# The first expert pass takes its tokens from SBUF by one-hot products, and constant products fill the routing waits

## The chip, the cores and the metric

One Trainium2 chip, one core. The time is the device time of the kernel in microseconds (us). On the core, TensorE (PE in the profile, its weight loads PEld) multiplies, VectorE (DVE), ScalarE (ACT) and GpSimd (POOL) do the rest, and SyncE (SP) issues most of the DMAs. TensorE's clock is granted at one of two levels, 1.2 or 2.4 GHz; the profile writes them as 0.50 and 1.00.

## What is computed

One layer for 512 tokens of width 1024, all in fp32: three branches (an RWKV-7 recurrence, a spatial gating unit, a convolution) are mixed, added to the input and normalised. Each token then goes to the two best of 32 experts.

```python
x = layer_norm(ALPHA * x + merged @ w_out[l], ln1_g[l], ln1_b[l])   # "x1" in the kernel
scores = sigmoid(x @ router_w)                                      # 512 x 32
# the best of 4 groups of 8 experts, in it the 2 best experts; gate = their scores, normed to 1
h = silu(xblk @ w_gate[e]) * (xblk @ w_up[e])                       # 1024 -> 512, for the tokens of expert e
y[token] += gate * (h @ w_down[e])                                  # 512 -> 1024
x = layer_norm(ALPHA * x + y, ln2_g[l], ln2_b[l])
```

## The kernel before

The program is written engine by engine, with semaphores, and each engine runs its instructions in the order in which they are written. The change touches the stretch between the branches and the experts, some 50 us long.

**Weights.** The experts' weights are 6 MB for each of 32 experts, cut into six chunks of 1 MB (four of gate and up, two of down). There are four sets of six places in SBUF; expert e uses set e mod 4. SP issues the loads in a fixed order. The loads of experts 0 to 3 (`load`, L410) go out as their places come free. The last four of them are chunks 0 and 1 of expert 3 (places in `ring`, where x1 lies too), which wait until x1 has been stored to DRAM (`x1_stored`), and chunks 4 and 5 of expert 2, which wait for the tables (`tables_ready`, s_tab). Behind them stands the loop of the other 28 experts (`reload`, L446): the chunk of expert e + 4 goes out when TensorE has used the same chunk of expert e (`w_used`).

**Residual, norm and router.** For each of four tiles c of 128 tokens TensorE forms the mixed rows (`mix`, L1372: 16 products of 512 columns), VectorE adds, normalises and leaves x1 in `ring` (L959 to L972), TensorE transposes it (`turn_x1`, L1381), ScalarE copies the transpose out of PSUM (L693) and stores x1 to DRAM, and TensorE forms the scores (`router`, L1388: 8 products of 32 columns). In the profile each fp32 product is two records of PE, each transpose one.

**Routing.** VectorE chooses the experts (L984 to L1010). TensorE then counts for each token how many before it chose the same expert (the rank products, L1409 and L1410). VectorE turns the ranks into pass and slot numbers (L1043 to L1064) and builds one-hot tables (L1070 to L1075). TensorE multiplies these (the table products, L1417), and VectorE writes the tables of token rows, result rows and gates (L1080 to L1082), which sets `tables_ready`.

**Passes.** A pass takes up to 64 tokens of one expert; there is one for each expert and one more for each further 64 tokens. GpSimd gathers the tokens of pass p from DRAM into `xe` by an indirect DMA (`gather`, L524 and L527), always one pass ahead. TensorE transposes them (`turn`, L1426), VectorE copies them to `xeT` (`turned`, L1095), TensorE does gate and up (L1437, 32 records), transposes of h (L1446) and down (L1457, 16 records), and GpSimd scatters the result (L541). The transposes of pass p + 1 stand on TensorE behind gate and up of pass p and ahead of the transposes of h. Pass 0 has its own `gather(0)` and `turn(0)`, and behind `turn(0)` TensorE reads the pass numbers of the first expert from SBUF (two register loads) and branches into the loop.

Of the kernel before, what the change touches and what calls it, by code (L numbers as in the profile page):

```python
# [10 lines left out]
ALU = mybir.AluOpType  # L11
ACT = mybir.ActivationFunctionType
AX_X = mybir.AxisListType.X
ADD, SUB, MUL, MAX = ALU.add, ALU.subtract, ALU.mult, ALU.max


P = 128
T, D = 512, 1024
KT = D // P
TT = T // P  # L20
# [135 lines left out]
def program(nc, x_tok, xT, w_in, par, table, lora, rows, sgu_b, sgu_wT, w_o, w_out, router_w, zeros, w_gu, w_down, out):  # L156
    with ExitStack() as ctx:
# [24 lines left out]
        def C(name):  # L182
            at, n = CONSTS[name]
            return const[:, at:at + n]
# [115 lines left out]
        def late(where, flat, n):  # L300
            at = place[where]
            place[where] += n
            return flat[:, at:at + n]
# [8 lines left out]
        slot_hot = late("late", late_sb, 8 * P).rearrange("p (n s) -> p n s", n=8)  # L312
        assert place["late"] <= 2 * RW + 2 * T
        chosen = late("raw", raw_flat, (TT + 1) * N_EXP).rearrange("p (c e) -> p c e", c=TT + 1)
        small = late("raw", raw_flat, 12 * TOPK * TT).rearrange("p (i n) -> p i n", i=12)
# [44 lines left out]
        s_begun, s_more = map(sem, ["gathers_begun", "further_passes_ready"])  # L360
        s_first, s_x1back, s_lnback = map(sem, ["first_passes_ready", "x1_back", "ln2_rows_in"])
        s_x1st, s_rw = sem("x1_stored"), sem("router_par_in")
# [13 lines left out]
        def _(sp):  # L376
# [54 lines left out]
            load(3, 3, 3)  # L431
            sp.wait_ge(s_x1st, 16 * TT)
            for c in (0, 1):
                load(3, c, 3)
# [35 lines left out]
        def _(pool):  # L470
# [51 lines left out]
            def gather(p):  # L522

                pool.tensor_copy(idx_now[:, 0:1], idx_tab[:, bass.ds(p, 1)]).then_inc(s_idx, 1)  # L524
                pool.wait_ge(s_idx, p + 1)
                pool.sem_inc(s_begun, 1)
                pool.indirect_dma_start(xe, None, x1_dram, bass.IndirectOffsetOnAxis(ap=idx_now[:, 0:1], axis=0),  # L527
                                        bounds_check=last_half_row, oob_is_err=False).then_inc(s_xe, 16)

            def next_tokens(p):  # L530
                pool.wait_ge(s_xe, p * 16 + 16)
                pool.wait_ge(s_xeTp, p + 1)
                gather(p + 1)
# [14 lines left out]

            gather(0)
            next_tokens(0)  # L550
            next_tokens(1)
# [9 lines left out]
            scatter(more + (N_EXP - 1))  # L561
            pool.wait_ge(s_xe, more * 16 + 16 * (N_EXP + 1))

# [165 lines left out]
        def _(dve):  # L729
# [280 lines left out]
            dve.tensor_tensor(chosen[:, 1:, :], hot[:, 0, :, :], hot[:, 1, :, :], ADD).then_inc(s_chosen, 1)  # L1010

            KC = TOPK * TT
            row_base = small[:, 0, 4:5]
# [26 lines left out]
            dve.wait_ge(s_rank, 1)  # L1040
            rank_ps = bank[:, 5, 0:TT * N_EXP].rearrange("p (c e) -> p c e", c=TT)
            for k in range(TOPK):
                ins = dve.tensor_tensor(work4[:, k, :, :], hot[:, k, :, :], rank_ps, MUL)  # L1043
# [19 lines left out]
            dve.tensor_copy(extra_i[:, :], count[:, EXTRA, :])  # L1063
            dve.tensor_copy(first_i[:, :], count[:, FIRST, :]).then_inc(s_first, 1)  # L1064


# [25 lines left out]

            def turned(p):
                dve.wait_ge(s_xeTp, p + 1)
                dve.tensor_copy(xeT, bank[:, 2, :].rearrange("p (c s) -> p c s", c=4)).then_inc(s_xeT, 1)  # L1095

            turned(0)
            with dve.Fori(0, N_EXP) as i:
# [36 lines left out]
        def _(pe):  # L1135
# [249 lines left out]
            def router(c):  # L1385
                pe.wait_ge(s_x1T, c + 1)
                for k in range(KT):
                    ins = pe.matmul(bank[:, 4, c * N_EXP:(c + 1) * N_EXP], x1T[:, c % 2, k, :], rw_sb[:, k, :],  # L1388
                                    start=(k == 0), stop=(k == KT - 1))
                if c == TT - 1:  # L1390
                    ins.then_inc(s_scp, 1)
# [4 lines left out]
            pe.wait_ge(s_m3, KT)  # L1396
            pe.wait_ge(s_rw, 32)
            for c in range(TT):
                if c + 1 < TT:
                    mix(c + 1)  # L1400
                if c:
                    router(c - 1)
                turn_x1(c)
            router(TT - 1)

            pe.wait_ge(s_chosen, 1)

            for n in range(TT + 1, 1, -1):
                pe.matmul(bank[:, 5, (TT + 1 - n) * N_EXP:(TT + 1) * N_EXP], C("ones"), chosen[:, 0:n, :], start=(n == TT + 1), stop=False)  # L1409
            pe.matmul(bank[:, 5, 0:TT * N_EXP], C("earlier"), chosen[:, 1:, :], start=False, stop=True).then_inc(s_rank, 1)  # L1410

            for n in range(TOPK * TT):
# [5 lines left out]
            ins.then_inc(s_tabp, 1)  # L1418
            pe.wait_ge(s_tab, 1)

            def turn(p):

                pe.wait_ge(s_xe, p * 16 + 16)
                pe.wait_ge(s_xeT, p)
                for c in range(4):
                    ins = pe.transpose(bank[:, 2, c * P:(c + 1) * P], xe[:, c * P:(c + 1) * P], C("ident"))  # L1426
                ins.then_inc(s_xeTp, 1)
# [34 lines left out]

            turn(0)
            pe.wait_ge(s_first, 1)
# [69 lines left out]
```

## Time and profile before

| | us |
|---|---|
| median of 3 runs | 1132.33 (1131.18 to 1133.24) |
| profiled execution | 1133.84 |
| its span, first to last instruction | 1132.1 |
| PE busy in the span | 990.2 (87%) |
| DVE busy | 359.3 (32%) |
| DMA: moved in the span | 261.35 MB, mean 231 GB/s |

What lies around the span is 1133.84 - 1132.1 = 1.74 us. Three things are to be read in the profile. The view by windows gives for a stretch how busy each engine was, the granted clock and what the DMA engines moved; where they move about 420 GB/s they are never idle. The chain of waits gives, back from the last instruction, what each piece waited for. The timeline gives each engine's instructions in order. An idle engine costs nothing unless the chain runs over it.

### The profile page before, as it was taken

How to read it: one execution, taken by the hardware profiler on the slowest of the kernel's cores; microseconds unless marked ns; L12 is line 12 of the kernel's file. 1: busy time of each engine (PE TensorE's matmuls, PEld its weight loads, DVE VectorE, ACT ScalarE, POOL GpSimd, SP SyncE). 2: the span in 40 equal slices, each digit the busy share in tenths (PEclk: the TensorE clock that was granted, in tenths of full speed). 3: DMA queues.
4: the chain of work that ended last, by engine and by line, in shares of the span. 5: the costliest groups of instructions: out<-in, count | busy, mean ns of one | idle time of the engine just before them, and what ended most of it. 6: DMA issues, size and time to landing. Idle time of an engine off the chain costs nothing.

```text
span 1132.1 us, 15272 instructions
## 1 busy us (share of the span) xinstructions
PE 990.2 (87%) x5900; PEld 458.8 (41%) x5901; DVE 359.3 (32%) x672; ACT 166.6 (15%) x302; POOL 123.9 (11%) x192
## 2 busy tenths in 40 slices
PE   7999999999999999999994588988888888887740
PEld 3634466466457447444454133333333333322210
DVE  0694452463363363322445000001100000000018
ACT  1113312321322132200000000000000100000010
POOL 1000010010010010033000112111211121111100
PEclk9999999999999999999995799999999999999985
DMA  8222211220220220573628699999999999999982
GB/s 252 61 74 56 75 39 39 58 55 20 75 57 21 56 56 2 171 297 153 258 83 344 219 416 419 403 419 420 419 419 420 419 419 419 419 420 420 421 322 117
DMA packets 90190, 261.35 MB, mean 231 GB/s; under 512 B 11080, under 2 KB 56136, under 8 KB 65312
## 3 DMA queue, kind: packets, MB, share of 16 engines
q1 hardware_dynamic: 83776, 249.46, 57.0%
q0 software_dynamic: 5648, 9.07, 2.2%
q10 hardware_dynamic: 720, 2.15, 0.5%
q8 instruction: 36, 0.59, 0.2%
q14 instruction: 10, 0.08, 0.0%
HBM read 256.97 MB, written 12.85 MB: 238 GB/s over the span
## 4 chain that ended last, share of the span: by engine, by line
PE 65%; DVE 15%; SPq 9%; DMA 5%; issue 4%; ACT 2%; DVEq 0%; ACTq 0%; POOLq 0%; PEldq 0%
PE bank L1437 14%; PE proj L1192 11%; SPq L446 9%; PE proj L1156 9%; PE bank L1457 7%; PE proj L1372 5%; PE bank L1282 5%; PE bank L1360 5%; DVE arena L760 4%; DMA arena<-w_gu 3%; DMA gates<-y_rows 2%; PE proj L1164 2%; DVE arena L1095 1%; DVE arena L845 1%; PE bank L1321 1%
## 5 line engine op out<-in xcount | busy, mean ns | idle before, releaser
L1192 PE MATMUL proj<-xT_sb,ring 128*128 128x512 f32 x384 | 182.1, 607 | 0.0
L1088 DVE TENSOR_TENSOR const<-pass_sb,bank 128x256 f32<-128x256 f32 x33 | 13.9, 422 | 408.3 <-ACT pass_sb L704 408.3
L1437 PE MATMUL bank<-arena 128*64 128x512 f32 x544 | 122.2, 596 | 15.7 <-PE bank L1457 11.1
L1156 PE MATMUL proj<-xT_sb,ring 128*128 128x512 f32 (+2 forms) x288 | 126.0, 594 | 0.0
L1192 PEld LDWEIGHTS proj<-xT_sb,ring 128*128 128x128 f32 x384 | 68.3, 189 | 68.3 <-issue 64.8
L1156 PEld LDWEIGHTS proj<-xT_sb,ring 128*128 128x128 f32 (+2 forms) x288 | 52.9, 185 | 71.6 <-issue 71.5
L1437 PEld LDWEIGHTS bank<-arena 128*64 128x64 f32 x544 | 43.0, 137 | 94.7 <-issue 82.8
L1437 PE MATMUL bank<-gates,arena 128*64 128x512 f32 x256 | 59.8, 617 | 8.6 <-PE bank L1457 4.7
L1282 PEld LDWEIGHTS bank<-arena 64*64 64x64 f32 x1536 | 52.8, 134 | 18.2 <-ACT arena L662 9.1
L1282 PE MATMUL bank<-arena 64*64 64x64 f32 (+1 forms) x1536 | 56.5, 228 | 0.0
L1360 PE MATMUL bank<-branches,arena 128*128 128x512 f32 x128 | 55.4, 593 | 0.9 <-DVE branches L939 0.9
L1457 PE MATMUL bank<-arena,const 128*64 128x512 f32 x208 | 48.4, 600 | 8.8 <-DVE const L1091 8.8
L1372 PE MATMUL proj<-arena 128*128 128x512 f32 x128 | 55.4, 592 | 0.0
L541 POOL DMA_INDIRECT y_rows<-const,raw x33 | 33.7, 1020 | 147.8 <-ACT const L708 147.8
L704 ACT ACTIVATE pass_sb<-bank 128x256 f32<-128x256 f32 x33 | 12.7, 384 | 249.5 <-PE bank L1437 249.5
L708 ACT ACTIVATE const<-bank,raw 128x512 f32<-128x512 f32 x33 | 22.7, 687 | 178.7 <-PE bank L1457 178.7
L760 DVE SCALAR_TENSOR_TENSOR arena<-arena,par_sb 128x512 f32<-128x512 f32 x60 | 39.8, 749 | 0.0
L527 POOL DMA_INDIRECT pass_sb<-x_rows,raw x34 | 35.8, 1052 | 26.9 <-POOL raw L524 24.6
L524 POOL COPY raw<-raw 128x1 int32 (+1 forms) x34 | 6.2, 183 | 296.4 <-PE bank L1426 207.2
L1437 PEld LDWEIGHTS bank<-gates,arena 128*64 128x64 f32 x256 | 18.5, 141 | 49.4 <-issue 43.2
L1360 PEld LDWEIGHTS bank<-branches,arena 128*128 128x128 f32 x128 | 24.2, 190 | 31.9 <-issue 30.1
L662 ACT ACTIVATE arena<-bank 128x256 f32<-128x256 f32 (+1 forms) x64 | 27.5, 437 | 64.6 <-PE bank L1282 59.6
(255 smaller groups left out, 1016.5 us busy)
## 6 DMA issues: line engine op xcount, KB each, us to landing
arena<-w_gu SPq DMA_DIRECT2D x64, 1024.0 KB, 24.6
gates<-w_gu SPq DMA_DIRECT2D x32, 1024.0 KB, 21.7
arena<-w_down SPq DMA_DIRECT2D x24, 1024.0 KB, 24.6
ring<-w_in SPq DMA_DIRECT2D x42, 512.0 KB, 3.9
gates<-w_down SPq DMA_DIRECT2D x16, 1024.0 KB, 23.6
branches<-w_down SPq DMA_DIRECT2D x16, 1024.0 KB, 26.7
xT_sb<-w_gu SPq DMA_DIRECT2D x16, 1024.0 KB, 26.0
ring<-w_gu SPq DMA_DIRECT2D x16, 1024.0 KB, 25.1
```

The costliest lines, as they stand in the source:

```text
L446: sp.dma_start(w_chunk[b][c], src.rearrange("a p n -> (a p) n")).then_inc(s_w[b][c], 16)
L527: pool.indirect_dma_start(xe, None, x1_dram, bass.IndirectOffsetOnAxis(ap=idx_now[:, 0:1], axis=0), bounds_check=last_half_row, oob_is_err ...
L541: pool.indirect_dma_start(y_dram, bass.IndirectOffsetOnAxis(ap=row_now[:, 0:1], axis=0), y_e, None, bounds_check=last_row, oob_is_err=Fals ...
L662: ins = act.activation(d, bank[:, 3 * g + b, 0:TT * n].rearrange("p (j n) -> p j n", j=TT), ACT.Copy)
L760: ins = dve.scalar_tensor_tensor(conv_acc[:, i, :], src, w, conv_acc[:, i, :], MUL, ADD)
L1156: ins = pe.matmul(proj[0:w, b, :], ring[:, slot, k, 0:w], xT_sb[:, k, :], start=(k == 0), stop=(k == KT - 1))
L1192: ins = pe.matmul(proj[:, gate_at["bank"], :], ring[:, gate_at["slot"], k, :], xT_sb[:, k, :], start=(k == 0), stop=(k == KT - 1))
L1282: ins = pe.matmul(bank[t, 3 * g + b, j * n:j * n + n], lhsT[t, j, :], rhs[t, j, :], start=True, stop=True)
L1360: ins = pe.matmul(bank[:, 3 * (m % 2) + n, :], wo_sb[:, k0 + k, m * P:(m + 1) * P], src[:, k, :], start=(k == 0), stop=(k == nk - 1))
L1372: ins = pe.matmul(proj[:, n % 2, :], merged[:, k, c * P:(c + 1) * P], wout_sb[:, k, T * i:T * i + T], start=(k == 0), stop=(k == KT - 1))
L1437: ins = pe.matmul(bank[SLOTS * h:SLOTS * h + SLOTS, 0, :], xeT[:, k % 4, SLOTS * (k // 4):SLOTS * (k // 4) + SLOTS], gu[k // 2][:, k % 2, ...
L1457: ins = pe.matmul(bank[SLOTS * h:SLOTS * h + SLOTS, 1, :], hT[:, f % 2, SLOTS * (f // 2):SLOTS * (f // 2) + SLOTS], wd[f // 2][:, f % 2, h ...
```

## The change

VectorE builds for each tile of 128 tokens a one-hot matrix `first_hot` (128 tokens by 64 slots) as soon as the rank products are there: a token has its one where its rank equals the slot, if it chose expert 0. TensorE multiplies x1, still in `ring`, by it: 8 blocks of 128 channels by 4 tiles, 32 products of 64 columns, which add up in the PSUM bank from which `turned(0)` copies. So `gather(0)`, `turn(0)` and TensorE's wait for the tables ahead of it are gone; `gather(1)` is the first. `turned(0)` moves on VectorE from behind the tables to a place ahead of the pass and slot one-hots, whose space `first_hot` shares. SP's loads of chunks 0 and 1 of expert 3, which overwrite x1, now also wait for the end of the new products (s_xeTp).

`keep_clock(n)` is n products of the identity by 512 constant columns into a free PSUM bank. There are 2 ahead of the last `turn_x1` (behind a wait for `residual_added`, since the bank holds mixed rows), 8 behind the last `router`, and 4 behind the new products.

```diff
+        first_hot = slot_hot[:, 6:8, :].rearrange("p n s -> p (n s)").rearrange("p (c s) -> p c s", c=TT)
...
             sp.wait_ge(s_x1st, 16 * TT)
+            sp.wait_ge(s_xeTp, 1)
             for c in (0, 1):
                 load(3, c, 3)
...
-                pool.wait_ge(s_idx, p + 1)
+                pool.wait_ge(s_idx, p)
...
-            gather(0)
-            next_tokens(0)
+            gather(1)
             next_tokens(1)
             scatter(0)
...
             rank_ps = bank[:, 5, 0:TT * N_EXP].rearrange("p (c e) -> p c e", c=TT)
+            for c in range(TT):
+                dve.tensor_scalar(first_hot[:, c, :], C("slot_iota")[:, 0:SLOTS], rank_ps[:, c, 0:1], chosen[:, 1 + c, 0:1],
+                                  ALU.is_equal, MUL).then_inc(s_firsthot, 1)
...
             dve.tensor_copy(first_i[:, :], count[:, FIRST, :]).then_inc(s_first, 1)
+            turned(0)
...
-            turned(0)
             with dve.Fori(0, N_EXP) as i:
...
+            def keep_clock(n):
+
+                for _ in range(n):
+                    pe.matmul(proj[:, 0, :], C("ident"), const[:, 0:T], start=True, stop=True)
+
             for c in range(TT):
                 if c + 1 < TT:
                     mix(c + 1)
                 if c:
                     router(c - 1)
+                if c == TT - 1:
+                    pe.wait_ge(s_pre, 2 * TT)
+                    keep_clock(2)
                 turn_x1(c)
             router(TT - 1)
+            keep_clock(8)
...
             pe.matmul(bank[:, 5, 0:TT * N_EXP], C("earlier"), chosen[:, 1:, :], start=False, stop=True).then_inc(s_rank, 1)
+
+            for c in range(TT):
+                pe.wait_ge(s_firsthot, c + 1)
+                for k in range(KT):
+                    at = (k % 4) * P + SLOTS * (k // 4)
+                    ins = pe.matmul(bank[:, 2, at:at + SLOTS], x1[:, c, k * P:(k + 1) * P], first_hot[:, c, :],
+                                    start=(c == 0 and k == 0), stop=(c == TT - 1 and k == KT - 1))
+            ins.then_inc(s_xeTp, 1)
+            keep_clock(4)
...
             ins.then_inc(s_tabp, 1)
-            pe.wait_ge(s_tab, 1)
...
-                pe.wait_ge(s_xe, p * 16 + 16)
+                pe.wait_ge(s_xe, p * 16)
...
-            turn(0)
             pe.wait_ge(s_first, 1)
```

TensorE from the last transposes of x1 to the passes, before (the number behind L is the line, `bank` and `proj` are PSUM, x counts instructions that read alike, and the brackets name the semaphores waited for):

```order
L1381 MATMUL bank<-const,ring 128x128 [waits x1T_out,x1_ready]
L1381 MATMUL bank<-const,ring 128x128 x7
L1388 MATMUL bank<-late_sb,xT_sb 128x32 [waits x1T_out]
L1388 MATMUL bank<-late_sb,xT_sb 128x32 x7
L1409 MATMUL bank<-raw,const 128x160 [waits chosen_ready]
...
L1410 MATMUL bank<-raw,const 128x128
L1417 MATMUL bank<-arena,late_sb 128x144 [waits scores_ready,one_hots_ready]
...
L1426 MATMUL bank<-const,pass_sb 128x128 [waits xeT_out,tokens_in,tables_ready]
L1426 MATMUL bank<-const,pass_sb 128x128 x3
L1477 UNCONDITIONAL_BRANCH [waits first_passes_ready]
```

The same place now (L1385, L1392, L1422, L1423 and L1439 are the old L1381, L1388, L1409, L1410 and L1417):

```order
L1405 MATMUL proj<-const 128x512 [waits residual_added]
L1405 MATMUL proj<-const 128x512
L1385 MATMUL bank<-const,ring 128x128 [waits x1T_out,x1_ready]
...
L1392 MATMUL bank<-late_sb,xT_sb 128x32 x7
L1405 MATMUL proj<-const 128x512 x8
L1422 MATMUL bank<-raw,const 128x160 [waits chosen_ready]
...
L1423 MATMUL bank<-raw,const 128x128
L1429 MATMUL bank<-late_sb,ring 128x64 [waits first_slots_ready]
...
L1405 MATMUL proj<-const 128x512 x4
L1439 MATMUL bank<-arena,late_sb 128x144 [waits scores_ready,one_hots_ready]
```

The new products (L1429) and the 4 fill products stand between the rank products and the table products, and no transposes of gathered tokens stand ahead of the branch any more.

SP's loads between the last router and the loop, before:

```order
L410 DMA xT_sb<-w_gu 128x2048 [waits scores_in_psum]
L410 DMA ring<-w_gu 128x2048 [waits x1_stored]
L410 DMA ring<-w_gu 128x2048
L410 DMA arena<-w_down 128x2048 [waits tables_ready]
L410 DMA late_sb<-w_down 128x2048
```

and now:

```order
L411 DMA xT_sb<-w_gu 128x2048 [waits scores_in_psum]
L411 DMA ring<-w_gu 128x2048 [waits xeT_psum,x1_stored]
L411 DMA ring<-w_gu 128x2048
L411 DMA arena<-w_down 128x2048 [waits tables_ready]
L411 DMA late_sb<-w_down 128x2048
```

The order of the loads is the same; the two of `ring` have one more wait.

## Rows read from the trace of the kernel before

**Rows 1.** Windows: start:end, length, busy us (x records), clock, DMA share, GB/s.

```profile
617.00:624.00 7.00, 4.19 (x16) 3.86 (x16) 3.56 (x12) 0.04 (x1) 0.00 (x0) 0.56 0.06 26
624.00:631.00 7.00, 0.00 (x0) 0.00 (x0) 0.00 (x0) 1.45 (x2) 1.32 (x2) 0.68 0.84 311
631.00:640.00 9.00, 5.81 (x16) 2.23 (x18) 0.69 (x1) 0.00 (x0) 1.24 (x2) 0.50 0.06 19
640.00:652.00 12.00, 10.26 (x48) 3.36 (x46) 1.38 (x3) 1.16 (x3) 1.44 (x4) 0.99 0.98 353
652.00:718.00 66.00, 58.45 (x272) 21.30 (x270) 6.88 (x15) 5.23 (x14) 12.25 (x20) 1.00 1.01 419
718.00:724.00 6.00, 6.00 (x31) 1.87 (x26) 0.00 (x0) 0.59 (x2) 1.01 (x1) 1.00 0.92 324
```

**Rows 2.** Timeline of TensorE: start, length, what, idle before it; first wait for weights.

```profile
1002.40 1.94 PE L1437 MATMUL bank<-arena 128*64 128x512 f32 x8 [0.34 <-DMA arena<-w_gu]
```

**Rows 3.** Timeline of SP's queue around routing and at expert 9's loads.

```profile
604.99 0.81 SPq L410 DMA_DIRECT2D ring<-w_gu  x2
623.88 0.33 SPq L410 DMA_DIRECT2D arena<-w_down  x1
...
639.15 7.19 SPq L446 DMA_DIRECT2D gates<-w_gu  x4
...
719.48 3.75 SPq L446 DMA_DIRECT2D arena<-w_gu  x3
```

**Rows 4.** Chain of waits, mixing to the third pass: start, us, what.

```profile
571.94 1.70 PE bank L1388 x16
...
574.55 13.75 PE proj L1372 x32
...
592.01 3.31 PE bank L1388 x16
595.33 1.77 PE bank L1381 x8
...
598.20 3.63 PE bank L1388 x16
...
609.74 2.08 PE bank L1409 x8
611.81 0.55 PE bank L1410 x2
...
616.56 0.47 DVE arena L1070
...
619.07 4.21 PE bank L1417 x16
...
623.87 8.46 issue
632.33 1.10 PE bank L1426 x4
...
633.45 0.70 DVE arena L1095
...
635.27 9.53 PE bank L1437 x32
...
651.20 7.10 PE bank L1437 x32
...
664.68 7.10 PE bank L1437 x32
```

**Rows 5.** Windows again, cut where the granted clock changes (columns as Rows 1).

```profile
588.00:592.40 4.40, 3.29 (x29) 2.92 (x27) 3.63 (x8) 1.16 (x2) 0.00 (x0) 1.00 0.71 249
592.40:616.00 23.60, 10.91 (x49) 10.08 (x48) 14.04 (x66) 2.58 (x3) 0.00 (x0) 0.50 1.01 417
...
623.10:626.50 3.40, 0.16 (x1) 0.00 (x0) 0.62 (x4) 1.49 (x2) 1.32 (x2) 1.00 0.45 101
```

**Rows 6.** Line 527, the 34 gathers of tokens, issue to landing.

```profile
DMA to landing us min/median/max: 3.4/6.7/7.6
```

More of the change, by code:

```diff
@@ L360, in program @@
         s_begun, s_more = map(sem, ["gathers_begun", "further_passes_ready"])
-        s_first, s_x1back, s_lnback = map(sem, ["first_passes_ready", "x1_back", "ln2_rows_in"])
+        s_firsthot, s_first, s_x1back, s_lnback = map(sem, ["first_slots_ready", "first_passes_ready", "x1_back", "ln2_rows_in"])
         s_x1st, s_rw = sem("x1_stored"), sem("router_par_in")
@@ L530, in next_tokens @@
             def next_tokens(p):
-                pool.wait_ge(s_xe, p * 16 + 16)
+                pool.wait_ge(s_xe, p * 16)
                 pool.wait_ge(s_xeTp, p + 1)
@@ L561, in _ @@
             scatter(more + (N_EXP - 1))
-            pool.wait_ge(s_xe, more * 16 + 16 * (N_EXP + 1))
+            pool.wait_ge(s_xe, more * 16 + 16 * N_EXP)
         @block.scalar
@@ L1010, in _, with turned @@
             dve.tensor_tensor(chosen[:, 1:, :], hot[:, 0, :, :], hot[:, 1, :, :], ADD).then_inc(s_chosen, 1)
+            def turned(p):
+                dve.wait_ge(s_xeTp, p + 1)
+                dve.tensor_copy(xeT, bank[:, 2, :].rearrange("p (c s) -> p c s", c=4)).then_inc(s_xeT, 1)
             KC = TOPK * TT
@@ L1091, in one_pass @@
                 dve.tensor_copy(hT, bank[:, 3, 0:FE // 2].rearrange("p (c s) -> p c s", c=2)).then_inc(s_hT, 1)
-            def turned(p):
-                dve.wait_ge(s_xeTp, p + 1)
-                dve.tensor_copy(xeT, bank[:, 2, :].rearrange("p (c s) -> p c s", c=4)).then_inc(s_xeT, 1)
-            turned(0)
             with dve.Fori(0, N_EXP) as i:
```

## The prediction

> **What bounds the kernel now.** I read three views in this order: the windows, to find where the DMA engines rest; the timelines of TensorE and of SP, to find who waits for whom in the passes; and the chain of waits, for the length of each step of the routing.
>
> From 652 us on the windows show 419 GB/s, which is as fast as this kernel's loads ever go; I call 420 full rate [rows 1]. TensorE waits for weights for the first time at 1002.40 us, and then in nearly every pass [rows 2]. Until then it is ahead, but its lead is only used up by a stream that never rests. So the end is set by the weights: bytes left, divided by 420 GB/s, plus every microsecond in which the DMA engines rest before the stream closes up. That is the quantity to sum. A TensorE that starts its passes earlier gains nothing by that itself; it gains by letting SP issue the reloads earlier.
>
> Rest before, as the missing part of each window: 617 to 624, 7 x (1 - 26/420) = 6.6; 624 to 631, 7 x (1 - 311/420) = 1.8; 631 to 640, 9 x (1 - 19/420) = 8.6; 640 to 652, 12 x (1 - 353/420) = 1.9. Together 18.9 us. Later there is one dip, 718 to 724: 6 x (1 - 324/420) = 1.4, where SP gets leave for expert 9's first chunk only at 719.48 [rows 1, 3]. All are TensorE's doing: the loads of `ring` go out at 604.99 and are through at about 617.4, the next two wait for the tables (623.88), and the first reload waits until the first pass has used its first chunk, at 639.15, 3.9 us after that pass began [rows 3, 4].
>
> **The change, step by step (times of the profiled execution).**
>
> 1. Two fill products ahead of the last transposes. A product of 512 columns is 13.75/16 = 0.86 us at 2.4 GHz (32 records are 16 products) and twice that, 1.72, at 1.2; the router shows the factor, 1.70 us for 16 records before the fall and 3.63 after it [rows 4]. The clock fell at 592.4 [rows 5], behind 4.1 us (the mixing ends at 574.55 + 13.75 = 588.3) in which TensorE did router products, transposes and a wait, and nothing of the change lies ahead of that. So the two products come cold, at 595.33, when the transposes could have gone: they cost 3.4 us on the chain. If they bring the clock back, the transposes (1.77) and the last router (3.63) halve, and 3.4 - 0.9 - 1.9 = +0.6 is left. Between +0.6 and +3.4 there is no row that decides: the one rise in this stretch came at 623.1, behind 4.0 us of table products, and these are 3.4 us. I take the middle, +2.0.
>
> 2. Eight fill products. The wait that hides them is 609.74 - 601.83 = 7.9 us (the last router ends at 598.20 + 3.63) [rows 4]. At 2.4 GHz they take 6.9 and are covered. If they start cold and the clock comes after about 4.4 us (4.0 us at the table products; in the first pass it came by about 640, some 4.8 us in), they take 4.4 + 4.7 = 9.1, so 1.2 are not covered. All cold: 13.7, which is rival B. The rank products then run at 2.4 GHz, 2.08 + 0.55 halved, -1.3. Ends for the rank products' end, 612.36 before: warm 0.6 - 1.3 = -0.7; cold 3.4 + 1.2 - 1.3 = +3.3. Middle +1.3: 613.7.
>
> 3. The new products. VectorE needs about 0.3 us for the first one-hot of 128 x 64 (an estimate, under the 0.47 of L1070's 128 x 384). 32 products are 64 records with a weight load of 128 x 128 each, as in the router; by its rows 64 x 1.70/16 = 6.8 us at 2.4 GHz and 64 x 3.63/16 = 14.5 at 1.2 [rows 4]. I take 6.8, as the eight fill products have just run: done at 613.7 + 0.3 + 6.8 = 620.8. VectorE's own chain to L1064 (612.36 to 616.56, plus under 1 us for the one-hots) lies beside it. The Trainium skill, TensorE: Matmul & The Clock Gate, section Back-to-back issue gap, gives about 81 ns for each matmul in a stream of weight loads and matmuls at 128 columns; no row here is that short (106 ns for 32 columns). By it the products would take 5.2 us and the forecast below would be 1.6 us lower.
>
> 4. VectorE now waits for them at `turned(0)`, and its pass and slot one-hots queue behind. From the end of the products: copy 0.7, then from L1070 to the table products, 619.07 - 616.56 = 2.5, so 3.2 us [rows 4]. The four fill products (3.4 us) lie beside this and end 0.2 later, at 624.2. The table products, 16 records in 4.21 at 1.2 GHz, take 2.1 at 2.4: end 626.3, tables ready 0.6 later at 626.9 (before 623.88, so 3.0 later).
>
> 5. The first pass. `gather(0)`, 8.46 us from tables to tokens, and `turn(0)`, 1.10, are gone [rows 4]. What stays is reading the pass numbers and branching: 635.27 - 633.43 = 1.8 us before, some of it perhaps beside the table products now; between 0 and 1.8 I take 0.9. Start 627.2 instead of 635.27: 8.1 us earlier. And warm: before, the first pass took 651.20 - 635.27 = 15.9 and the second 664.68 - 651.20 = 13.5, so 2.4 less [rows 4]. But its last part waits for `gather(1)`, which only starts at the tables: 626.9 + 8.5 = 635.4, against 627.2 + 7.1 = 634.3, some 1.0 us late. TensorE is then 8.1 + 2.4 - 1.0 = 9.5 us ahead of the old trace in all later passes. The landing times (3.4 to 7.6, median 6.7) [rows 6] leave up to 0.9 more wait.
>    The Trainium skill, DMA: Bandwidth & Descriptors, section Anatomy of one DMA, gives about 2.0 us plus bytes/436 GB/s for a DMA of GpSimd; 0.26 MB would be 2.6 us, and `gather(1)` would land before it is wanted. The trace says 6.7 [rows 6]; by the page the forecast would be about 0.5 lower.
>
> 6. The DMA engines. The two `ring` loads (2.1 MB, 5.0 us) leave their old place, so the queue is dry at 617.4 - 5.0 = 612.4. They now go out at 620.8, and bytes flow some 1.6 us behind an issue (1.8 us of rest in 624 to 631, the window that begins at the issue of 623.88 [rows 1, 3]): rest 622.4 - 612.4 = 10.0. They are through at 627.4; the next two, issued at 626.9, flow at 628.5: 1.1 more. They last till 633.5, and the first reload is issued 653.31 - 651.20 = 2.1 us into a warm pass, at 629.3: no more rest. Total 11.1 instead of 18.9, and 0.6 us of work less (one gather of 0.26 MB): the stream is 8.4 us ahead. At expert 9 SP gets leave at 719.48 - 9.5 = 710.0, and the queue runs dry at about 719.4 - 8.4 = 711.0; before, the two coincided. With the 1.6 us of flow some 0.6 of the dip is left: 0.8 more. Sum 9.2 us.
>
> Own time of the profiled execution 1133.84 - 9.2 = 1124.6 (span 1122.9); it stood 1.5 above the median 1132.33, so the median is **1123.1**. With the warm end of steps 1 and 2 everything after is 2.0 earlier, 1121.1; with the cold end 1125.1.
>
> **The rivals.**
>
> A. The clock falls again within the new products: half the time of each of their records is weight load, and the fall at 592.4 came behind 4.1 us of like work [rows 5]. Against it: those 4.1 us held waits and transposes, and the new products follow eight dense ones without a gap. If it falls 4 us in, the other 2.8 double (+2.8) and the four fill products start cold (+2.2). Products end 623.6, tables 631.9; rest 12.8 + 3.3 = 16.1; stream ahead 18.9 - 16.1 + 0.6 = 3.4, dip 0.7: **1128.2**.
>
> B. The other side: the fill fails to raise the clock, or not before the new products. The place is the eight fill products: at 1.2 GHz they take 13.7 against a cover of 7.9, and nothing behind them on TensorE can pass. With all cold: rank products end 612.36 + 3.4 + 5.8 = 621.6, the new ones 636.4, then 6.9 and 4.2: tables 648.1, rest 25.6 + 6.7 = 32.3: **1145**. If only the new products are cold (+7.7, fill +2.5): rest 17.7 + 3.6, **1133** to 1135. It decides where the new products end later than about 630 (620.8 + 9.2). For it: the clock stood at 1.2 from 592.4 to 623.1 with 11 of 23.6 us busy [rows 5]. Against it: table products and gate/up products did raise it.
>
> C. It does not do what it says, as the DMA engines are not earlier: the loads of `ring`, held until x1 is used, rest as long as the gather did. This is the sum of step 6 with another end, and it needs the products to end after 629: TensorE would be ahead and the stream would not. **1131** to 1132.
>
> **How the numbers follow.** Main case 0.70: 1123.1, its own range 1121 to 1125 widened by 0.5 for the dip, the branch and the gather. A 0.14, 1128. C, with the cold-products half of B, 0.07, 1131 to 1134. B, slower, 0.09, 1135 to 1145. The range 1120.5 to 1129.5 takes in the main case and A. A measurement of this kernel can tell 0.2% (2.3 us) from no change: faster (under 1130.1) 0.84, same 0.07, slower 0.09.
>
> **What would show it.** In the new profile: two L1405 products between 595 and 599 that delay the transposes; the clock back at 2.4 before the rank products; L1429, 64 records in about 7 us, ending at 619 to 623; the first pass at about 627, 7.1 us long in gate and up; a short wait ahead of the transposes of pass 1; DMA rest between 612 and 622 and none between 631 and 640; the dip at 720 nearly gone; first wait for weights still near 1000. It would be wrong if L1429 takes over 10 us, if the first pass starts after 632, or if the DMA engines rest a second time behind 630.

## The result, and the profile after

The change makes the kernel 0.5% faster: 1127.67 us, the median of 7 times from 1122.5 to 1131.47, against 1132.09, the median of 7 from 1130.62 to 1133.24; the ratio is 0.995 with a 95% interval of 0.993 to 0.9971. That is 4.4 us, half of the 9.2 forecast. It is inside the stated range, but outside the main case's own range of 1121 to 1125: the median falls in a group that the range takes in only because it was drawn wide enough for rival A. That it hit the range is luck. The times of the changed kernel are not spread evenly. They lie in three groups, and the mean granted clock of each execution goes with them: three at 1122.5 to 1123.8 (clock 0.981), three at 1127.7 to 1127.9 (0.976 to 0.977), one at 1131.5 (0.973). The profiled execution took 1123.78 us with a span of 1122.0, so it belongs to the first group: it shows the change at its best, 10.1 us under the span before.

TensorE's timeline in it (start, length, what, idle before it):

```profile
591.71 1.97 PE L1392 MATMUL bank<-late_sb,xT_sb 128*128 128x32 f32 x16 [1.11 <-ACT xT_sb L694]
593.51 3.30 PE L1405 MATMUL proj<-const 128*128 128x512 f32 x4
596.61 1.43 PE L1385 MATMUL bank<-const,ring 128*128 128x128 f32 x8
599.15 2.13 PE L1392 MATMUL bank<-late_sb,xT_sb 128*128 128x32 f32 x16 [1.11 <-ACT xT_sb L694]
601.09 8.67 PE L1405 MATMUL proj<-const 128*128 128x512 f32 x16
609.60 1.05 PE L1422 MATMUL bank<-raw,const 128*128 128x160 f32 x8
...
611.50 7.36 PE L1429 MATMUL bank<-late_sb,ring 128*128 128x64 f32 x64 [0.58 <-DVE late_sb L1048]
618.70 3.65 PE L1405 MATMUL proj<-const 128*128 128x512 f32 x8
622.19 2.14 PE L1439 MATMUL bank<-arena,late_sb 128*128 128x144 f32 x16
626.02 7.09 PE L1458 MATMUL bank<-gates,arena 128*64 128x512 f32 x32 [1.69 <-issue]
633.88 0.66 PE L1447 MATMUL bank<-const,pass_sb 128*128 128x128 f32 x4 [0.78 <-DMA pass_sb<-x_rows,raw]
```

Against [rows 4]: the first pass starts at 626.02 instead of 635.27 and its gate and up take 7.1 us instead of 9.5; its transposes wait 0.78 us for the gather. The new products (L1429) take 7.4 us. SP's queue in the same execution:

```profile
618.96 0.80 SPq L411 DMA_DIRECT2D ring<-w_gu  x2
624.95 0.33 SPq L411 DMA_DIRECT2D arena<-w_down  x1
...
628.15 6.50 SPq L448 DMA_DIRECT2D gates<-w_gu  x4
...
708.37 6.51 SPq L448 DMA_DIRECT2D arena<-w_gu  x4
```

And its windows (columns as in [rows 1]):

```profile
612.00:620.00 8.00, 8.00 (x65) 7.33 (x65) 4.97 (x20) 0.00 (x0) 0.00 (x0) 1.00 0.07 19
620.00:624.00 4.00, 4.00 (x21) 2.66 (x20) 2.98 (x8) 0.00 (x0) 0.00 (x0) 1.00 0.94 354
624.00:628.00 4.00, 2.31 (x13) 0.91 (x13) 0.62 (x4) 1.49 (x2) 1.32 (x2) 1.00 0.88 295
628.00:640.00 12.00, 9.63 (x46) 3.19 (x43) 1.44 (x3) 1.03 (x3) 1.43 (x3) 1.00 1.01 421
640.00:708.00 68.00, 60.57 (x278) 23.48 (x280) 6.89 (x15) 5.94 (x17) 12.28 (x20) 1.00 1.02 418
```

There is one hole left in the DMA stream, 612 to 620, where [rows 1] had two, 617 to 624 and 631 to 640. From 628 on it is closed. The first reload is issued at 628.15, 11.0 us earlier than in [rows 3], and expert 9's at 708.37 instead of 719.48.

### The profile page after: what moved, and what is told of

Read it like the earlier page. It is cut to its first block, busy times and chain, and to the rows that moved or that the text cites. A ratio compares the mean times of both kernels' runs of the same rounds, so it can differ in the third digit from the quotient of the medians.

```text
span 1122.0 us, 15417 instructions
## 1 busy us (share of the span) xinstructions
PE 1001.1 (89%) x5988; PEld 469.4 (42%) x5989; DVE 360.3 (32%) x676; ACT 166.4 (15%) x302; POOL 122.6 (11%) x190
## 4 chain that ended last, share of the span: by engine, by line
PE 68%; DVE 15%; DMA 6%; SPq 6%; issue 3%; ACT 2%; DVEq 0%; POOLq 0%; POOL 0%; ACTq 0%
PE bank L1458 16%; PE proj L1196 11%; PE proj L1160 9%; PE bank L1478 9%; SPq L448 5%; PE proj L1376 5%; PE bank L1286 5%; PE bank L1364 5%; DVE arena L761 4%; DMA arena<-w_gu 3%; DVE arena L1015 2%; DMA gates<-y_rows 2%; PE proj L1168 1%; DVE arena L846 1%; ACT pass_sb L705 1%
## 5 line engine op out<-in xcount | busy, mean ns | idle before, releaser
L1097 DVE TENSOR_TENSOR const<-pass_sb,bank 128x256 f32<-128x256 f32 x33 | 13.9, 421 | 406.8 <-ACT pass_sb L705 406.8
L1458 PE MATMUL bank<-arena 128*64 128x512 f32 x544 | 122.9, 595 | 16.3 <-PE bank L1478 11.1
L1458 PEld LDWEIGHTS bank<-arena 128*64 128x64 f32 x544 | 48.0, 136 | 90.9 <-issue 75.5
L1458 PE MATMUL bank<-gates,arena 128*64 128x512 f32 x256 | 57.4, 596 | 8.4 <-PE bank L1478 4.8
L705 ACT ACTIVATE pass_sb<-bank 128x256 f32<-128x256 f32 x33 | 12.7, 383 | 237.8 <-PE bank L1458 237.8
```

The lines of the kernel that those rows point to most:

```text
L1458: ins = pe.matmul(bank[SLOTS * h:SLOTS * h + SLOTS, 0, :], xeT[:, k % 4, SLOTS * (k // 4):SLOTS * (k // 4) + SLOTS], gu[k // 2][:, k % 2, ...
```

## The measure behind all runs: the rest of the stream

For each profiled execution I took the missing part of two windows, 60 x (1 - GB/s / 420) from 600 to 660 us and 40 x (1 - GB/s / 420) from 700 to 740, as the prediction did in its sum. The rows of before, of the changed kernel and of the run no_fill, one fence each:

```profile
600.00:660.00 60.00, 32.00 (x131) 16.31 (x130) 19.64 (x85) 3.31 (x7) 5.18 (x9) 0.69 0.73 289
700.00:740.00 40.00, 35.35 (x165) 12.83 (x166) 4.65 (x11) 3.49 (x9) 7.80 (x13) 1.00 1.00 407
```

```profile
600.00:660.00 60.00, 53.73 (x263) 29.05 (x264) 20.80 (x89) 4.48 (x10) 6.23 (x10) 0.97 0.87 354
700.00:740.00 40.00, 35.81 (x166) 12.64 (x162) 4.13 (x9) 3.48 (x9) 7.35 (x12) 1.00 1.01 415
```

```profile
600.00:660.00 60.00, 44.83 (x199) 29.44 (x201) 20.77 (x89) 3.31 (x7) 5.21 (x9) 0.70 0.70 282
700.00:740.00 40.00, 35.77 (x168) 12.82 (x166) 4.13 (x9) 3.48 (x9) 7.36 (x12) 1.00 1.01 419
```

| kernel | span, us | rest, us | span - rest | first reload issued |
|---|---|---|---|---|
| before | 1132.1 | 18.7 + 1.2 = 19.9 | 1112.2 | 639.15 |
| changed | 1122.0 | 9.4 + 0.5 = 9.9 | 1112.1 | 628.15 |
| again | 1125.0 | 12.4 + 0.3 = 12.7 | 1112.3 | 631.27 |
| no_fill | 1132.5 | 19.7 + 0.1 = 19.8 | 1112.7 | 636.87 |
| fill_only | 1132.2 | 18.3 + 1.5 = 19.8 | 1112.4 | 638.61 |
| gap_fill | 1127.0 | 14.0 + 0.8 = 14.8 | 1112.2 | 631.46 |
| no2 | 1120.6 | 9.1 + 0.2 = 9.3 | 1111.3 | 626.75 |
| no8 | 1135.4 | 21.9 + 2.2 = 24.1 | 1111.3 | 638.91 |
| no4 | 1130.5 | 17.6 + 0.8 = 18.4 | 1112.1 | 635.34 |
| gap_fill2 | 1119.5 | 7.6 + 0.4 = 8.0 | 1111.5 | 625.81 |

Three more runs, told of below, fit in: bridge 1125.2 - 13.0 = 1112.2, no2_bridge 1123.9 - 11.1 = 1112.8, gap_fill2b 1119.4 - 8.0 = 1111.4. These are thirteen profiled executions with spans from 1119.4 to 1135.4, and the difference stays within 1111.3 to 1112.8; what makes up this 1.5 us was not looked into. Outside the two windows there is nothing to add: from 740 to 1060 us all thirteen moved 420 GB/s. So each microsecond in which the DMA engines rest behind 600 us comes back in the span. The last column alone would not do: no_fill issues its first reload 2.3 us before the old kernel and is no faster.

## The experiments

All change the PE program only; the tokens, weights and results are the same as in the changed kernel unless a run says otherwise. A fill product changes nothing that is read.

**again.** No edit.

> The changed kernel once more, unaltered. Its seven times lie in three groups: 1122.5 to 1123.8 with a mean granted clock of 0.981, 1127.7 to 1127.9 with 0.976, and 1131.5 with 0.973. Theory (the time depends on when in the routing the clock falls and rises again, and that differs between executions): the new times fall into the same groups again, the higher the time the lower the clock, about 5 us for each 0.005 of mean clock, and if the profiled execution is of a slower group, its trace shows part of the new one-hot products or of the 8 fill products at 1.2 GHz and the first reload of weights later by what the time is longer. Rival (the groups are noise of the DMA stream): the clock column doesn't go with the time, and the stream moves under 418 GB/s behind 652 us in a slow one.

Measured: median 1127.12 of 12, before 1131.72; three times at 1122.2 to 1122.8 (clock 0.981), four at 1126.5 to 1127.5 (0.976 to 0.977), five at 1129.1 to 1132.2 (0.972 to 0.975). The groups come back and the clock goes with them. With the first seven: 6 of 19 up to 1124, 7 from 1126 to 1128, 6 over 1129. No execution of the upper group was profiled, in this run or the first; what is said of it below rests on its time, its mean clock and the traces of gap_fill and no4. The profiled execution, 1126.72, is of the middle group:

```profile
591.60 3.56 PE L1392 MATMUL bank<-late_sb,xT_sb 128*128 128x32 f32 x16 [1.11 <-ACT xT_sb L694]
594.97 3.72 PE L1405 MATMUL proj<-const 128*128 128x512 f32 x4
...
600.68 2.50 PE L1392 MATMUL bank<-late_sb,xT_sb 128*128 128x32 f32 x16 [1.11 <-ACT xT_sb L694]
603.00 9.97 PE L1405 MATMUL proj<-const 128*128 128x512 f32 x16
...
614.62 7.36 PE L1429 MATMUL bank<-late_sb,ring 128*128 128x64 f32 x64 [0.48 <-DVE late_sb L1048]
```

Its windows, cut where the clock changes:

```profile
592.00:598.50 6.50, 6.50 (x19) 4.35 (x20) 2.16 (x4) 0.00 (x0) 0.00 (x0) 0.50 1.01 396
598.50:602.00 3.50, 2.39 (x21) 2.13 (x19) 0.00 (x0) 2.31 (x2) 0.00 (x0) 0.99 1.00 420
602.00:608.80 6.80, 6.80 (x13) 3.50 (x13) 4.73 (x31) 0.28 (x1) 0.00 (x0) 0.50 1.02 430
```

The clock fell at 591.7 here, and at 594.0 in the first group's execution. So router and first fill ran cold (3.56 and 3.72 against 1.97 and 3.30), the clock fell again at 602.0, and the eight fills took 9.97 us instead of 8.67. The new products start 3.1 us later and so does all that follows: 3.0 us of span. These two executions differ by where the fall lies in a program that is the same. The rival is out: behind 660 us the stream moved 418 to 420 GB/s in both.

**no_fill.**

```diff
-                if c == TT - 1:
-                    pe.wait_ge(s_pre, 2 * TT)
-                    keep_clock(2)
...
-            keep_clock(8)
...
-            keep_clock(4)
```

> The changed kernel without any of the 14 fill products: the one-hot products alone. Theory (the new products need a warm clock and don't make one before they are done): they run at 1.2 GHz, 64 records in 14.5 us instead of 7.4, end at about 627, the tables come at 635, the first pass starts at 636 like before, and the time is 1131 to 1133, no gain against before. Rival (unbroken one-hot products raise the clock themselves after some 4.4 us, as the table products did after 4.0): 4.4 us cold and the rest warm, 9.2 us in all, first pass at about 629, time about 1125, as good as with the fill.

Measured: median 1132.5 of 12, before 1131.72, ratio 1.0005 (0.9996 to 1.0014). No gain, as the theory had it. TensorE's timeline in no_fill:

```profile
612.51 13.91 PE L1425 MATMUL bank<-late_sb,ring 128*128 128x64 f32 x64 [0.49 <-DVE late_sb L1048]
629.66 4.21 PE L1434 MATMUL bank<-arena,late_sb 128*128 128x144 f32 x16 [3.24 <-DVE late_sb L1084]
633.80 8.03 PE L1453 MATMUL bank<-gates,arena 128*64 128x512 f32 x32
...
986.55 1.94 PE L1453 MATMUL bank<-arena 128*64 128x512 f32 x8 [0.30 <-DMA arena<-w_gu]
```

The windows of the new products and of what follows in the same execution:

```profile
610.00:626.40 16.40, 15.91 (x74) 15.45 (x72) 5.89 (x27) 0.00 (x0) 0.00 (x0) 0.50 0.12 50
626.40:635.50 9.10, 5.86 (x21) 4.40 (x22) 4.70 (x13) 0.94 (x1) 0.18 (x1) 0.50 0.64 238
```

The new products ran 13.9 us at 1.2 GHz without a gap and the clock did not come back in them; it came at 635.7. Yet TensorE was ahead of the old kernel: first pass 1.5 us earlier and partly warm. It ran into its first wait for weights at 986.6, 16 us earlier than in [rows 2], and the lead bought nothing, since x1 held the `ring` loads back until 626.5 and the stream rested as long as before.

**fill_only.** The kernel before with the same three fills (the 4 behind the rank products).

```diff
+                if c == TT - 1:
+                    pe.wait_ge(s_pre, 2 * TT)
+                    keep_clock(2)
                 turn_x1(c)
             router(TT - 1)
+            keep_clock(8)
...
+            keep_clock(4)
```

> The kernel before with the 2, 8 and 4 fill products alone, at the same places (the 4 behind the rank products); tokens of pass 0 are gathered as before. Theory (the fill pays only as a preparation for work of TensorE, and the gather wait of 8.5 us leaves the engine idle and the clock low again): rank products 1.4 us shorter, table products perhaps 2.1 shorter, first pass cold again; time 1.4 to 3.5 us under before, 1128.6 to 1130.7. Rival (the clock is most of the gain of the change): the first pass is warm too and the time is at 1127 or lower.

Measured: median 1131.76 of 12, before 1131.72, ratio 0.9995 (0.9986 to 1.0004). Less than either view expected: no gain. TensorE's timeline in fill_only:

```profile
603.13 9.93 PE L1401 MATMUL proj<-const 128*128 128x512 f32 x16
...
620.94 2.23 PE L1427 MATMUL bank<-arena,late_sb 128*128 128x144 f32 x16 [3.28 <-DVE late_sb L1075]
631.79 1.09 PE L1436 MATMUL bank<-const,pass_sb 128*128 128x128 f32 x4 [8.63 <-issue]
634.73 9.45 PE L1447 MATMUL bank<-gates,arena 128*64 128x512 f32 x32 [1.85 <-issue]
```

The warm table products end at 623.2, as in [rows 4] at 623.3: what they gain is what the two cold fills ahead of the transposes had cost. The gather wait of 8.6 us lets the clock fall, and the first pass is cold again. So neither half of the change does anything alone; the products need the fill, and the fill needs the products.

**no8.**

```diff
             router(TT - 1)
-            keep_clock(8)
```

> The changed kernel without the 8 fill products behind the last router; 2 and 4 stay. In the run no_fill 64 one-hot records took 13.9 us at 1.2 GHz and did not raise the clock. Theory (the 8 are what makes the new products warm): the clock is low from the idle wait on, the new products take 14 us and end at about 626 to 629, the first pass starts at about 635, and the median is 1131 to 1134: the whole gain is gone. Rival (the warmth comes from the 2 ahead): the median stays at 1127.

Measured: median 1134.89 of 12 (five from 1130.3 to 1131.9, seven from 1134.5 to 1137.1), before 1131.71, ratio 1.0017 (1.0004 to 1.003), 0.2% slower, the only kernel whose interval lies above before. That is more than the 1131 to 1134 expected. Its profiled execution is of the upper group. TensorE's timeline in it:

```profile
614.32 13.92 PE L1428 MATMUL bank<-late_sb,ring 128*128 128x64 f32 x64 [0.48 <-DVE late_sb L1048]
628.02 6.14 PE L1405 MATMUL proj<-const 128*128 128x512 f32 x8
634.00 2.12 PE L1438 MATMUL bank<-arena,late_sb 128*128 128x144 f32 x16
```

Behind cold products the 4 fills are cold too and take longer than the 3.2 us that VectorE needs for its one-hots (no_fill): the table products start at 634.00, where in no_fill they start at 629.66, and the first pass at 636.06 instead of 633.80.

**no2.**

```diff
-                if c == TT - 1:
-                    pe.wait_ge(s_pre, 2 * TT)
-                    keep_clock(2)
                 turn_x1(c)
             router(TT - 1)
+            pe.wait_ge(s_pre, 2 * TT)
             keep_clock(8)
```

> The changed kernel without the 2 fill products ahead of the last transposes; 8 and 4 stay. In the run again the 2 took 3.7 us cold and gave back 0.9 at the transposes and 1.1 at the last router, so the scores came 1.6 us or more later than they would without. Theory (the 2 fill products are a loss of 1 to 2 us): the last transposes and router run cold (1.8 and 3.6), the scores come 1 to 2 us earlier than in again, the 8 then raise the clock, and the median is 1124 to 1126.5. Rival (they are needed, since the 8 alone raise the clock too late): more of the 8 run cold, past the end of VectorE's choice, and the median is 1127 or above.

Measured: median 1122.77 of 5, from 1121.7 to 1124.0, before 1131.71, ratio 0.9921 (0.9908 to 0.9934). Better than the theory expected, and in five times none of the two slower groups. TensorE's timeline in no2:

```profile
596.19 3.62 PE L1392 MATMUL bank<-late_sb,xT_sb 128*128 128x32 f32 x16 [1.11 <-ACT xT_sb L694]
599.63 8.84 PE L1405 MATMUL proj<-const 128*128 128x512 f32 x16
```

The last router is cold, 3.62, and still the eight fills start at 599.63, against 601.09 and 603.00 in the two traces of the changed kernel. Some of that is not the edit's doing, since the mixing ended 1.2 us earlier in this execution. Counted from its end the fills start 12.9 us behind it, against 13.1 and 15.1. So where the clock falls early the two fills ahead of the transposes cost some 2 us more than they give back, and where it falls late next to nothing: the median, 1122.77, is that of the changed kernel's first group.

**no4.**

```diff
             ins.then_inc(s_xeTp, 1)
-            keep_clock(4)
```

> The changed kernel without the 4 fill products behind the new ones; 2 and 8 stay. TensorE then waits some 3.2 us for VectorE's one-hots with nothing to do. Theory (the 4 are hidden and hold the clock over this wait): the new products end as before, but in part of the executions the table products (2.0 warm, 4.2 cold) and the first pass (7.1 warm, 9.5 cold) run at 1.2 GHz, so the first reload is up to 2 to 3.5 us later and the median is 1127 to 1130. Rival (the wait is too short to lose the clock): same as again, 1127, or 0.3 below.

Measured: median 1127.74 of 5 (1124.7, 1125.2, 1127.7, 1128.6, 1132.2), before 1131.71, ratio 0.9953 (0.994 to 0.9967). The median doesn't tell the two views apart. The profiled execution is the slowest: it lost the clock within the new products (11.4 us, from 616.3 on), and the table products, 3.24 us behind them, took 4.21 cold. The two lowest times lie 1 to 3 us above the changed kernel's first group; what the 4 fills are worth where the clock holds stays open.

**gap_fill.** The two fills go from ahead of the last transposes into the two waits for ScalarE's copies.

```diff
-                if c == TT - 1:
-                    pe.wait_ge(s_pre, 2 * TT)
-                    keep_clock(2)
                 turn_x1(c)
+                if c >= TT - 2:
+                    pe.wait_ge(s_pre, 2 * TT)
+                    keep_clock(1)
```

> The changed kernel with the 2 fill products ahead of the last transposes taken away and put one each into the two waits of 1.1 us in which ScalarE copies the transposes (behind the transposes of tiles 2 and 3); 8 and 4 stay. Theory (the 2 cost 3.1 us on the chain, most of which the warmer router doesn't give back): in the gaps they are hidden when warm (0.86 against 1.1 us); if the clock then holds at 2.4 GHz, the scores come 3 us earlier than in the changed kernel and the time is 1119 to 1121. Rival (the clock falls all the same, as the router products and transposes are too light): the fills take 1.7 us cold, 0.6 over the gap each, the last router 3.6, and the time is 1122 to 1126.

Measured: median 1123.58 of 6 (1120.5, 1123.3, 1123.4, 1123.8, 1128.7, 1128.9), before 1131.72, ratio 0.9926 (0.9905 to 0.9947). The last router ends 11.6 us behind the mixing (13.3 and 15.3 in the two traces of the changed kernel), so the scores are earlier, but the kernel is slower than the theory's figure: in the profiled execution, one of the two slow ones, the clock is lost within the new products. TensorE's timeline in it:

```profile
609.93 12.12 PE L1429 MATMUL bank<-late_sb,ring 128*128 128x64 f32 x64 [0.87 <-DVE late_sb L1048]
621.85 5.51 PE L1405 MATMUL proj<-const 128*128 128x512 f32 x8
```

And its windows, cut where the clock fell:

```profile
598.50:611.90 13.40, 11.57 (x55) 7.20 (x54) 10.84 (x60) 0.28 (x1) 0.00 (x0) 1.00 1.01 426
611.90:625.50 13.60, 13.60 (x54) 11.53 (x54) 5.76 (x20) 0.00 (x0) 0.00 (x0) 0.50 0.21 70
```

This is rival A of the prediction, seen: 12.1 + 5.5 us where the first trace has 7.4 + 3.7.

**gap_fill2 and gap_fill2b.** gap_fill with 9 fills behind the last router and 1 between the rank products and the new ones.

```diff
-            keep_clock(8)
+            keep_clock(9)
...
             pe.matmul(bank[:, 5, 0:TT * N_EXP], C("earlier"), chosen[:, 1:, :], start=False, stop=True).then_inc(s_rank, 1)
+            keep_clock(1)
```

> The kernel of the run gap_fill with 9 fill products instead of 8 behind the last router and 1 more between the rank products and the new products. There TensorE was idle for 0.96 us ahead of the rank products and 0.87 us behind them, the clock fell at 611.9, 2 us into the new products, and these took 12.1 us instead of 7.4. Theory (the light stretch around the rank products is where the clock is lost): both waits are filled, nothing on the chain gets longer by over 0.2 us, the clock is lost less often, and the median is 1120.5 to 1122.5, with few times over 1126. Rival (the new products themselves are too light, and the clock falls within them in the same share of executions): median and spread as for gap_fill, 1123 to 1125.

> gap_fill2 again, to see how often it loses the clock (so far 4 times at 1120.9 to 1121.3, one at 1124.5). Theory: median 1121 to 1122, at most one time in five over 1124.

Measured: 1121.25 (four from 1120.9 to 1121.3, one 1124.5), before 1131.71, ratio 0.9912 (0.9899 to 0.9925); again 1121.07 (four from 1120.7 to 1121.2, one 1124.6), before 1132.34, ratio 0.9909 (0.9894 to 0.9924). Both theories on it held. This is the best version found, 10.5 to 11.3 us under before, 6 under the change as made. The two times at 1124.5 go with a mean clock of 0.979, the other eight with 0.982; neither was profiled. TensorE's timeline in gap_fill2, the first of the two:

```profile
597.01 1.95 PE L1392 MATMUL bank<-late_sb,xT_sb 128*128 128x32 f32 x16
598.79 7.97 PE L1405 MATMUL proj<-const 128*128 128x512 f32 x18
606.87 1.15 PE L1422 MATMUL bank<-raw,const 128*128 128x160 f32 x8
...
608.13 1.02 PE L1405 MATMUL proj<-const 128*128 128x512 f32 x2
609.16 7.36 PE L1430 MATMUL bank<-late_sb,ring 128*128 128x64 f32 x64
```

No idle time stands before any of these rows, and the new products start 2.3 us earlier than in the first trace of the changed kernel (0.7 of it because the mixing ended earlier).

**bridge** and **no2_bridge.** The changed kernel with that one fill behind the rank products alone, and no2 with it and 9 for 8.

> The changed kernel with one more fill product between the rank products and the new ones, nothing else. The 19 times of the changed kernel so far: 6 up to 1124, 7 from 1126 to 1128, 6 from 1129 to 1132. Theory (the times over 1129 are executions in which the clock is lost within the new products, since the engine is idle or light around the rank products): the group over 1129 goes or shrinks to one in ten, the other two stay, median about 1126. Rival (the new products lose the clock whatever stands ahead): the same three groups, median 1127.

> The changed kernel without the 2 fill products ahead of the last transposes, 9 instead of 8 behind the last router, 1 between the rank products and the new ones, and the 4. It parts gap_fill2 (1121.3) into its pieces: if the two fills in the gaps matter, this is slower than gap_fill2 by about what the transposes and the last router lose cold (0.9 + 1.5 us): 1122.5 to 1123.5, like no2 (1122.8); if only the fill behind the router and around the rank products matters, 1121 to 1122.

Measured: bridge 1124.81 of 6, three at 1122.6 to 1122.7 and three at 1126.9 to 1127.1, none above; before 1132.34, ratio 0.9933 (0.9916 to 0.995). The two lower groups stay and the upper does not show; with 6 of 19 before, six times in a row without it would come by luck in one case of ten. no2_bridge 1124.37 of 5 (1122.9 to 1125.6), ratio 0.9928 (0.9915 to 0.9941): over what was expected, and not better than no2. In its trace the clock fell at 591.8, before router 2, and came back at 605.5; in that of no2 it fell at 592.9 and came at 603.1. The fills in the gaps are worth some 3 us (gap_fill2 against no2_bridge, which differ in them alone); in the traces of gap_fill2 the clock fell at 593.8 and was back at 597.2.

Of the upper group, then: the kernels that are idle around the rank products with fills ahead of the transposes or in the gaps (changed, again, gap_fill) lost the clock within the new products, by time and mean clock, in 8 of 25 executions, one of them traced; the four runs with a fill there in 0 of 21. no4, also without it, lost it in its traced execution. no2, without it, did not lose it in 5 either. The fill behind the rank products is what I take to hold the clock, with that reservation: only bridge adds it alone, and gap_fill2 also has the ninth fill ahead of the rank products; why the same program loses it in one execution in three and not in the others no trace here shows.

## Why the prediction was right, and where it was wrong

**What bounds the kernel.** Right: span minus rest is the same to within 1.5 us in all profiled executions, and no_fill showed the point on which the argument turned, that TensorE can be ahead and gain nothing. TensorE's first wait for weights in the changed kernel moved with the rest, to 992.05 (timeline):

```profile
992.05 1.94 PE L1458 MATMUL bank<-arena 128*64 128x512 f32 x8 [0.53 <-DMA arena<-w_gu]
```

**Step 1, two fills ahead of the transposes.** Here the prediction failed in its form. It had two ends, +0.6 and +3.4, and took the middle, +2.0. The executions do not lie between the ends: they split. From the end of the mixing to the end of the last router before took 601.83 - 588.30 = 13.5 us; in the first trace after it is 13.3 (-0.2), in again 15.3 (+1.8). The time of the likeliest case was to be forecast, and the middle of two groups is the time of neither.

**Step 2, eight fills.** In the first trace they end 0.4 us behind VectorE's choice, in again 1.8 behind it (1.2 was forecast for a cold start). The clock came back 3.1 us after the start of these fills in the first trace and 5.8 in again, not 4.4. Together with step 1 the two groups' new products start 3.1 us apart; the forecast had its ends 4.0 apart.

**Step 3, the new products.** 7.4 us where 6.8 was forecast, in both traces of the changed kernel. In its third group, by time and mean clock, the clock is lost in them: rival A, given 0.14, would be 6 of 19. Its price was taken from the middle case, 1128.2; seen, the group lies at 1129 to 1132, and gap_fill's two at 1128.7 and 1128.9. This is the second part of the error: with the middle group, 13 of 19 executions lie above the main case's 1125.

**Steps 4 and 5.** The table products end 5.5 us behind the new ones (5.5 forecast), the tables 0.6 later. Reading the pass numbers leaves TensorE idle for 1.69 us, not 0.9. It does lie in part beside the table products, which are too short when warm (2.1 us) to cover it: in no_fill and no4, where they took 4.2 us, and in no8 and gap_fill, where the fills ahead of them were cold, no idle time stands ahead of the first pass. The wait for the gather was 0.78 (1.0 forecast). The formula of the Trainium skill, DMA: Bandwidth & Descriptors, section Anatomy of one DMA, weighed there, would have had no such wait; `gather(1)` took 8.9 us from the tables to the transposes, so the trace was the better guide. So too for the new products: by the 81 ns of the Trainium skill, TensorE: Matmul & The Clock Gate, section Back-to-back issue gap, they would take 5.2 us; they took 7.36, 115 ns for each of 64 records.

**Step 6.** The forecast holes, 612.4 to 622.4 and one of 1.1, are those seen, the first 2 us shorter as its warm end has it: 19 GB/s from 612 to 620, 295 from 624 to 628, and full rate from 628. The dip at expert 9 shrank from 1.2 to 0.5 (0.6 forecast to be left). The warm execution's span was forecast at 1132.1 - 11.2 = 1120.9 and is 1122.0. Of the 1.1 more some 0.5 is the work of the gather that is gone, put at 0.6, of which span - rest shows 0.1 (1112.2 and 1112.1); the rest before was put 0.4 too high (20.3, measured 19.9) and the rest after 0.2 too low (9.7, measured 9.9). The branch is no term of it: the first pass began later than forecast, and the DMA engines were full again from 628 all the same. The cold one's span was forecast at 1132.1 - 7.2 = 1124.9, and is 1125.0.

**The base.** The profiled execution of before, 1133.84, lies 1.7 above the later median of 1132.09 (57 later times of before lie between 1130.3 and 1134.4). Subtracted from the median, a sum that is right for that trace is too large by some of this: the cold case counted from 1133.84 gives 1126.6, and again's profiled execution took 1126.72; counted from the median 1132.33, as the prediction did, it gives 1125.1. What that execution had longer was not looked into.

**The rivals.** B happened in no8: slower than before, 14 us for the new products. Its price for that case, 1133 to 1135, is what was measured, 1134.9. C, in no_fill: the stream no earlier, 1132.5. For A the prediction argued that half the time of each record is weight load; the windows show weight loads for 7.33 of the 8.00 us from 612 to 620, and the clock held there.

## What to carry to other kernels

When a later stage is bound by a stream of loads, sum the time in which the stream rests, not the time in which an engine is ahead; a step that frees an engine and holds a buffer longer may give nothing. Constant products on TensorE pay where they stand in waits that are there anyway, up to the length of the wait; ahead of work that is ready they can cost more than a warmer engine gives back, as the two ahead of the transposes did where the clock fell early. If a step's price depends on the clock, forecast the two cases and their shares, not their mean, and time the kernel often enough to see the groups.

## What the runs showed of the hardware

TensorE can be busy without a gap and stay at 1.2 GHz: the new products ran 13.9 us so, and the clock did not come back in them (no_fill, and 13.92 us in no8). In the fill products behind the last router it came back (at 604.2 in the first trace, where they began at 601.09, at 608.8 from 603.00 in again). And the same program's time differs by 10 us between executions (1122.2 to 1132.2, mean clock 0.981 to 0.972), where before it differed by 4; the traces of two of its three groups show the clock as what differs.
